# Feed-forward activations turned in blocks of 32 by 32 and moved through DRAM, instead of transposed on TensorE

## What is computed

```python
h = rmsnorm(x, norm_ffn_g[l])
x = x + (jax.nn.silu(h @ w_gate[l]) * (h @ w_up[l])) @ w_down[l]
return rmsnorm(x, norm_final_g)
```

## Time and profile before

| | |
|---|---|
| median of 3 runs | 1132.21 us (1132.09 to 1132.76) |
| the profiled execution | 1132.04 us |
| its span, first to last instruction | 1130.2 us |
| TensorE busy | 1116.9 us, 99% of the span |
| VectorE busy | 714.2 us, 63% |
| ScalarE busy | 532.6 us, 47% |
| share of the 16 DMA engines, q1 | 60.8% |
| granted TensorE clock | 0.998 of full speed |

### The profile page before, as it was taken

How to read it: one execution, slowest core, us unless ns; L and a number is a source line. 1 busy time by engine, 2 the same in 40 slices (tenths; PEclk the granted TensorE clock), 3 DMA queues, 4 the chain that set the end, 5 groups by cost and what they waited for, 6 DMA issues and landing times.

```text
span 1130.2 us, 15159 instructions
## 1 busy us (share of the span) xinstructions
PE 1116.9 (99%) x5618; PEld 925.8 (82%) x5618; DVE 714.2 (63%) x783; ACT 532.6 (47%) x640; POOL 88.3 (8%) x130
## 2 busy tenths in 40 slices
PE   9999999999999999999999999999999999999996
PEld 7878778888988888888888888888888888888885
DVE  7999998566765645464555546455554645556466
ACT  7569444345734553434343443444434343443443
POOL 7120234220000000000000000000000000000000
PEclk9999999999999999999999999999999999999999
DMA  9883688854665567566665656656566666656652
GB/s 362 285 237 115 203 247 261 229 170 149 237 210 197 171 204 215 188 192 186 191 198 186 188 188 195 188 188 196 187 192 186 191 190 193 188 186 201 186 187 93
DMA packets 115095, 224.81 MB, mean 199 GB/s; under 512 B 8432, under 2 KB 13936, under 8 KB 114416
## 3 DMA queue, kind: packets, MB, share of 16 engines
q1 hardware_dynamic: 110832, 214.05, 60.8%
q0 software_dynamic: 3808, 9.31, 3.2%
q10 hardware_dynamic: 416, 0.92, 0.2%
HBM read 218.09 MB, written 5.11 MB: 197 GB/s over the span
## 4 chain that ended last, share of the span: by engine, by line
PE 86%; DVE 8%; DMA 2%; issue 1%; ACT 1%; SPq 0%; POOL 0%; POOLq 0%; DVEq 0%; ACTq 0%
PE ps L1404 24%; PE ps L1406 24%; PE ps L1405 24%; PE ps L1442 3%; PE ps L1435 3%; PE ps L1439 3%; DVE w_lo L778 3%; DMA raw<-in_w_in 2%; PE ps L1651 1%; PE ps L1720 1%; PE ps L1722 1%; PE ps L1721 1%; PE ps L1550 0%; DVE cl_t L978 0%; DMA swapped<-state 0%
## 5 line engine op out<-in xcount | busy, mean ns | idle before, releaser
L778 DVE TENSOR_TENSOR w_lo<-raw,w_hi 128x1024 fp32r<-128x1024 f32 x384 | 467.8, 1224 | 383.0 <-ACT w_hi L442 382.0
L442 ACT ACTIVATE w_hi<-raw 128x1024 fp32r<-128x1024 f32 x383 | 406.0, 1061 | 563.8 <-PE ps L1406 456.2
L1404 PE MATMUL ps<-w_hi,actA_hi 128*128 128x512 f32 x416 | 162.9, 392 | 0.0
L1405 PE MATMUL ps<-w_lo,actA_hi 128*128 128x512 f32 x416 | 161.9, 389 | 0.0
L1406 PE MATMUL ps<-w_hi,actA_lo 128*128 128x512 f32 x416 | 161.9, 389 | 0.0
L1406 PE MATMUL ps<-w_hi,h2B_lo 128*128 128x512 f32 x352 | 137.0, 389 | 0.0
L1404 PE MATMUL ps<-w_hi,h2B_hi 128*128 128x512 f32 x352 | 136.9, 389 | 0.0
L1405 PE MATMUL ps<-w_lo,h2B_hi 128*128 128x512 f32 x352 | 136.9, 389 | 0.0
L1404 PE MATMUL ps<-w_hi,ffT_hi 128*128 128x512 f32 x320 | 124.6, 389 | 0.0
L1406 PE MATMUL ps<-w_hi,ffT_lo 128*128 128x512 f32 x320 | 124.5, 389 | 0.0
L1405 PE MATMUL ps<-w_lo,ffT_hi 128*128 128x512 f32 x320 | 124.5, 389 | 0.0
(11 more groups left out here) (265 smaller groups left out, 1294.1 us busy)
## 6 DMA issues: line engine op xcount, KB each, us to landing
raw<-in_w_gate SPq DMA_DIRECT2D x88, 512.0 KB, 3.7
raw<-in_w_up SPq DMA_DIRECT2D x88, 512.0 KB, 3.7
raw<-in_w_down SPq DMA_DIRECT2D x88, 512.0 KB, 3.6
raw<-in_w_in SPq DMA_DIRECT2D x79, 512.0 KB, 5.4
raw<-in_w_out SPq DMA_DIRECT2D x32, 512.0 KB, 4.3
k_tab<-k_scratch POOLq DMA_DIRECT2D x64, 64.0 KB, 3.7
raw<-in_ssm_w_glu SPq DMA_DIRECT2D x8, 512.0 KB, 3.4
x_tok<-in_x_tok SPq DMA_DIRECT2D x2, 1024.0 KB, 8.5
```

What stands on the lines that cost most here:

```text
L442: nc.scalar.activation(w_hi[:, s % SPL], raw[:, s % RAW], ACT.Copy).then_inc(S["high_done"], 1)
L778: tt(w_lo[:, s % SPL], raw[:, s % RAW], w_hi[:, s % SPL].bitcast(F32), ALU.subtract).then_inc(S["low_done"], 1)
L1404: mm(o, x_hi, h, start=first, stop=False)
L1405: mm(o, x_hi, l, start=False, stop=False)
```

## The change

The ten transpositions inside the loop leave TensorE. VectorE transposes `ff_act` within squares of 32 x 32 (`turn_blocks`: two instructions of 128 x 512, one for each half of the tokens) into `ff_turned`. SyncE stores `ff_turned` to a DRAM scratch (512 KB) behind the load of chunk 5, and loads it back in eight pieces of 64 KB, one behind each load of chunks 8 to 15, so that each 32 x 32 square ends on the partitions on which it belongs (`ff_moved`). `ffT_high` and `ffT_low` read `ff_moved` in SBUF in place of PSUM. `ffT_high` now stands behind `high` of chunk 17, and `ffT_low` behind `low` of chunk 18. `turn_blocks` stands behind `low` of chunk 20. The eleventh group is still transposed by TensorE.

```diff
+        ff_dram = nc.dram_tensor("ff_scratch", (P, TOK * NCOL), F32, kind="Internal").ap()
...
+        moved_view = ff_moved[:].rearrange("p t a k j -> p (t a) k j")
+        def turned_view(x):
+            return x.rearrange("p k (c j) -> p c k j", j=32)
...
                     load(LOOP0 + c, src.rearrange("(b p) n -> p b n", p=P), turn=j)
+                    if c == 5:
+                        sp.wait_ge(S["turned"], j + 1)
+                        sp.dma_start(ff_dram, ff_turned[:].rearrange("p b t k j -> p (b t k j)")).then_inc(d_parked, 16)
+                    if 8 <= c < 16:
+                        sp.wait_ge(d_parked, (j + 1) * 16)
+                        b, t = divmod(c - 8, TOK)
+                        sp.dma_start(ff_moved[32 * b:32 * b + 32, t].rearrange("p a k j -> p a (k j)"),
+                                     ff_dram.rearrange("(a p) (b t m) -> b t p a m", a=4, b=4, t=TOK)[b, t]
+                                     ).then_inc(d_moved, 16)
...
             def ffT_high(count):
-                act.wait_ge(S["ffT_mm"], count)
-                nc.scalar.activation(ffT_hi[:].rearrange("p (a b) s -> p a (b s)", a=2), ps[:, 4:6], ACT.Copy
+                act.wait_ge(d_moved, count * MOVED)
+                nc.scalar.activation(turned_view(ffT_hi[:]), moved_view, ACT.Copy
                                      ).then_inc(S["ffT_hi_ready"], 1)
...
                     high(None, turn=j, at=LOOP0 + c)
                     if c == GRP + SPL - 1:
+                        act.wait_ge(S["turned"], j + 1)
+                        silu(j * TURN + (LOOP0 + GRP))
+                    if c == GRP + SPL + 5:
                         ffT_high(j + 1)
-                        silu(j * TURN + (LOOP0 + GRP))
...
+            def turn_blocks(count, moved):
+                dve.wait_ge(S["ff_ready"], count)
+                if moved is not None:
+                    dve.wait_ge(d_moved, moved)
+                for t in range(TOK):
+                    last = nc.vector.transpose(ff_turned[:, :, t].rearrange("p b k j -> p k b j"),
+                                               ff_act[:, t].rearrange("p (k b j) -> p k b j", k=4, b=4))
+                last.then_inc(S["turned"], 1)
...
             def ffT_low(count):
                 dve.wait_ge(S["ffT_hi_ready"], count)
-                tt(ffT_lo[:].rearrange("p (a b) s -> p a (b s)", a=2), ps[:, 4:6],
-                   ffT_hi[:].rearrange("p (a b) s -> p a (b s)", a=2).bitcast(F32), ALU.subtract
-                   ).then_inc(S["ffT_lo_ready"], 1)
+                tt(turned_view(ffT_lo[:]), moved_view,
+                   turned_view(ffT_hi[:]).bitcast(F32), ALU.subtract).then_inc(S["ffT_lo_ready"], 1)
...
                 if n == LOOP0 + 3:
                     ff(1, LOOP0)
+                    turn_blocks(1, None)
...
                     low(None, turn=j, at=LOOP0 + c)
-                    if c == GRP + 3:
+                    if c == GRP + SPL + 6:
                         ffT_low(j + 1)
                     if c == 2 * GRP + 3:
                         ff(j + 2, j * TURN + (LOOP0 + 2 * GRP))
+                    if not last and c == 2 * GRP + 4:
+                        turn_blocks(j + 2, (j + 1) * MOVED)
...
                     if c == GRP - 1:
                         pe.wait_ge(S["cols_added"], j * 4 + 8)
-                        ff_transposes(j + 1)
```

More of the change, by code:

```diff
@@ L127 @@
 SQUARES_AT = 8
+MOVED = 8 * 16
 LAST_ORDER = tuple((t, slice(NCOL * c, NCOL * (c + 1))) for c, t in ((0, 0), (0, 1), (1, 0), (1, 1), (2, 0), (3, 0), (2, 1))
@@ L176, in build @@
         x2, state, swapped, kT, warm = (m[k] for k in ("x2", "state", "swapped", "kT", "warm"))
-        m = overlay([("qT", [P, HEADS, SEQ], F32)], [("u_tok", [P, TOK, 1024], F32)],
+        m = overlay([("qT", [P, HEADS, SEQ], F32)], [("ff_turned", [P, 4, TOK, 4, 32], F32), ("ff_moved", [P, TOK, 4, 4, 32], F32)], [("u_tok", [P, TOK, 1024], F32)],
                     [("cosA", [P, HALF, NCH], F32), ("sinA", [P, HALF, NCH], F32)])
@@ L181, in build @@
         ret = qT
+        ff_turned, ff_moved = m["ff_turned"], m["ff_moved"]
         m = overlay([("u_loc", [P, GROUPS, NCH], F32)],
@@ L276, in build @@
             "zT_ready sqT_ready ssm_hi ssm_lo sq_added ssq_mm ssq_ready cols_added last_added h2_mm h2_hi h2_lo x2_sq silu_ready ff_ready "
-            "ffT_mm ffT_hi_ready ffT_lo_ready fin_sq gain_done fin_ready fin1_ready last_mm"
+            "turned ffT_mm ffT_hi_ready ffT_lo_ready fin_sq gain_done fin_ready fin1_ready last_mm"
         ).split()
+        d_moved = sem("d_moved")
+        d_parked = sem("d_parked")
         S = {n: sem(n) for n in names}
@@ L727, in turn @@
                     if c == GRP + SPL - 1:
+                        act.wait_ge(S["turned"], j + 1)
+                        silu(j * TURN + (LOOP0 + GRP))
+                    if c == GRP + SPL + 5:
                         ffT_high(j + 1)
-                        silu(j * TURN + (LOOP0 + GRP))
                     if last and c == 2 * GRP + 8:
-                        act.wait_ge(S["ffT_mm"], FG)
+                        act.wait_ge(S["ffT_mm"], 1)
                         nc.scalar.activation(ffE_hi[:].rearrange("p (a b) s -> p a (b s)", a=2), ps[:, 0:2], ACT.Copy
```

## The result

| | before | after |
|---|---|---|
| median, 16 runs each | 1132.33 us | 1135.45 us (1134.46 to 1136.4) |
| ratio of the two | | 1.0026, 95% interval 1.0019 to 1.0033 |
| profiled execution | 1132.04 us | 1134.54 us |
| its span | 1130.2 us | 1132.7 us |
| TensorE busy | 1116.9 us | 1111.2 us |

The kernel is 0.26% slower, +2.9 us by the ratio, +2.5 us between the profiled executions; 1134.5 had been predicted, 2.3 us over the kernel before. The interval leaves out 1.0000, so the loss is there; its lower end, 1.0019, lies just under the 0.2% that the prediction took as the least that can be told from no change.

What follows compares the result with a forecast made beforehand. TensorE was taken to bound the kernel, never pausing in the loop. 10 x (1.13 - 0.895) = +2.35 us on 1132.21 us gave 1134.5 us; range 1133.3 to 1138.5, forecast alone 1133.5 to 1135.3 (chance 0.70).

Steps and rivals of the forecast that it cites:

- What is removed: In the loop, eight transpositions a turn leave TensorE: 0.895 us a turn gained, 8.95 us for 80.
- What is moved: Ahead of chunk 16, TensorE waits 1.13 us a turn for `ffT_low` behind `low` 18: 11.3 us lost in ten turns.
- TensorE's restart: After `ffT_low` ends, the stream runs as if its first matmul stood 0.18 us later; 0.02 added for long first steps.
- What is added: In the loop, `ffT_high` from SBUF, VectorE's pair (0.7 to 2.3 us) and nine more SyncE transfers a turn, all hidden.
- SyncE's wait in the first turn: At the store in SyncE's queue, `turned` was claimed satisfied five chunks before it is asked, at no cost.
- The dearer layout (1): Runs of 32 elements make `ffT_low` 0.2 to 0.4 us dearer: 1136.5 to 1138.5 us; chance 0.11.
- Double rate (2): `ffT_low`'s subtraction from SBUF runs at double rate and ends 0.53 us earlier: 1129.2 us; chance 0.07.
- Slow transpositions (3): VectorE's pair takes 4.6 us; from 3.0 us on, `down_col` is late at chunk 20: 1150 us; chance 0.06.
- Late transfers (4): Small pieces or the store delay weight loads beyond 4.9 us; 0.5 us a turn beyond gives 1139.5 us; chance 0.06.
- the bound: For the whole kernel, 0.2% (2.26 us) is the least distinguishable from no change: 1134.47 us.

Runs made afterwards that it cites:

- The version one chunk earlier: Changed kernel with `ffT_high` behind `high` of chunk 16 and `ffT_low` behind `low` of chunk 17: 1123.48 us, ratio 0.9921.
- the run with more work for VectorE: Changed kernel with `ffT_high` and `ffT_low` one chunk earlier, plus four more VectorE transpositions into an unused tile in `turn_blocks`: 1126.59 us, ratio 0.9946.

## Why the prediction was right

**What is removed: right.** 0.895 us a turn was read from distances between starts, not from durations. The version one chunk earlier gives a turn of 65.29 us and 8.9 us in all. The durations in the records would have said 22 us, and the 390 ns of the Trainium skill (VectorE: DVE Perf Modes, The three transpose paths), as an estimate, 31; no run agrees with either.

**What is moved: right in kind and place, 0.06 us short in size.** The order `high` 18, `low` 18, `ffT_low` within one chunk came as derived, with `ffT_low` at 1217 ns. The term that was mis-sized is TensorE's restart. It had been taken as 0.05 us from the end of VectorE's instruction to TensorE's start, from one wait of an early stage. In the loop `ffT_lo` ends at 613.15 and TensorE starts with its weight load at 613.27, 0.12 later; the stream then runs as from 0.25 after the end, where 0.18 and 0.02 were added. Hence 1.19 against 1.13, 0.6 us over ten turns. The sum with it: 10 x (1.19 - 0.895) = 2.95, and the ratio gives 2.9.

The restart is not one number. A weight load in the loop, then `ffT_lo` and the weight load of the tenth turn, in the profile after:

```profile
613.27 0.19 PEld L1441 LDWEIGHTS ps<-w_hi,ffT_hi 128*128 128x128 f32 x1 [1.32 <-issue]
```
```profile
1077.26 1.22 DVE L1133 TENSOR_TENSOR ffT_lo<-ff_moved,ffT_hi 128x1024 fp32r<-128x1024 f32 x1
1078.53 0.19 PEld L1441 LDWEIGHTS ps<-w_hi,ffT_hi 128*128 128x128 f32 x1 [1.31 <-DVE ffT_lo L1133]
```

The tenth turn has the same matmuls and waits, but stands outside the loop, and there the load starts 0.05 after the end (1078.48), as the prediction had it. Ahead of chunk 20 in the run with more work for VectorE it is 0.06, and that is in the loop. In the program a second wait, for the chunk's weights, follows the wait for `ffT_lo`, while the wait for `down_col` stands right ahead of the load. So the 0.07 us more may be that second wait, whose count in the loop depends on the turn. This is argued from the program; no run tried it.

**What is added: right that it is hidden, with one oversight.** 0.65 us for a transposition, where 0.74 was taken. The figure of the Trainium skill (same page and section) for bf16, 311 ns a square, had given as an estimate 1.24 for four of them; measured are 0.69 for all four in float32. One square by itself was not run. The oversight is SyncE's wait in the first turn. `high` 6 started 2.7 us late (4.33 of idle time where 1.66 is usual), 3.1 us were left, and it cost nothing here.

**The rivals.** The dearer layout (1): no, 1217 ns. Double rate (2): no, the same figure. Slow transpositions (3): the mechanism exists and sits where it was placed, as six of them showed, but two are far from it. Late transfers (4): the median load landed up to 1.1 us later, and outside the hold of the first turn none kept ScalarE waiting in the loop.

**The chances.** The forecast lay on the bound, and so does the result: 1.0026 with an interval from 1.0019. The median, 1135.45, stands 0.15 us above the 1133.5 to 1135.3 that the forecast was given by itself. It lies in the part of the stated range that had been added for rival 1, and rival 1 did not come. So the range held here partly by luck: the terms make 0.6 us of the excess over the forecast, the kernel before was 0.1 slower here than in the three runs of the prediction, and the rest is no more than the spread of the runs.

## What to carry to other kernels

When a step is moved in the queue of an in-order engine, count what stands ahead of it there and what that work waits for: here `ffT_low` inherited, through `low` and `high` of chunk 18, a wait for TensorE itself, and one place in a queue was worth 12 us while all the new work was worth nothing. Put the consumer's operand as many steps ahead of its use as the rest of the pipeline has (here one more was enough), and when a change takes work off the bound engine and the time does not fall, look for the new pause before doubting the saving.

## What the runs showed that was not expected

A pause of TensorE has two prices. At 1.2 us a turn it cost its length and the granted clock stayed at 1.00; at 2.4 us the clock fell to 0.50 for a few microseconds behind four pauses of ten, at 1.6 us each; at 3.9 us each turn lost 2.4 us on average beyond the wait. Transpositions of 128 x 512 in float32 on VectorE take 0.67 to 0.71 us and start 0.60 us apart in a row. A plain pass over 1024 elements is followed by the next after 1.14, so that 512 would be, as an estimate, 0.57: about the same price.
